# Weight halves at a step of 132 words, and matmuls that stream and write their columns from the last to the first

## The reference, cut to what matters

```python
# first block, per layer (DEPTH = 2)
proj = jnp.einsum('btd,de->bte', h, w_in[l])
c_out = ... jnp.einsum('btc,cd->btd', y, w_pw)
x = x + jnp.einsum('btd,de->bte', merged, w_out[l])
gu = jnp.einsum('btd,df->btf', h2, w_gate_up[l])
x = x + jnp.einsum('btf,fd->btd', jax.nn.silu(g) * up, w_down[l])
# second block
proj = h @ w_in
... (o * jax.nn.silu(g)) @ w_ret_o ; y @ w_sgu_o ; merged @ w_out
... h @ w_up ; conv ; (jax.nn.gelu(a) * b) @ w_down
```

## Time and profile before

| | |
|---|---|
| runs | 2197.36 and 2197.77 us, median 2197.57 |
| profiled execution | span 2195.6 us from the first to the last instruction; some 2.0 us of the runs' time lie around it |
| PE | 2182.7 us busy (99%), 10528 matmuls |
| PEld | 1813.8 us (83%) |
| DVE | 1378.5 us (63%) |
| ACT | 965.5 us (44%) |
| DMA | 27% of the 16 engines, 95 GB/s |
| granted TensorE clock | 0.999 of full speed |

### The profile page before, as it was taken

The page is one execution under the profiler, slowest core; times in us unless marked ns, Lnnn a source line. Parts: engine busy times, 40 slices in busy tenths (PEclk is TensorE's granted clock), DMA queues, the critical chain, the costliest instruction groups (busy, mean ns, idle before and its releaser), DMA issues.

```text
span 2195.6 us, 28930 instructions
## 1 busy us (share of the span) xinstructions
PE 2182.7 (99%) x10528; PEld 1813.8 (83%) x10528; DVE 1378.5 (63%) x1978; ACT 965.5 (44%) x1392; POOL 74.7 (3%) x103
## 2 busy tenths in 40 slices
PE   9999999999999999999999999999999999999998
PEld 6878888888888878888888888888888899888887
DVE  7999954444345999954444334654776568888723
ACT  5678544443223588544443223331554344333412
POOL 0000020000010000020000010000000000000000
PEclk9999999999999999999999999999999999999999
DMA  5221222222223211222222224223222231222222
GB/s 182 75 78 65 96 96 96 96 96 84 93 93 123 90 62 64 94 96 100 99 99 92 80 92 156 97 77 131 84 91 87 96 135 39 100 101 97 94 96 77
DMA packets 35397, 208.39 MB, mean 95 GB/s; under 512 B 4512, under 2 KB 5024, under 8 KB 14816
## 3 DMA queue, kind: packets, MB, share of 16 engines
q1 hardware_dynamic: 35296, 207.07, 27.0%
HBM read 201.15 MB, written 2.10 MB: 93 GB/s over the span
## 4 chain that ended last, share of the span: by engine, by line
PE 94%; ACT 3%; DVE 2%; issue 1%; DMA 0%; SPq 0%; DVEq 0%
PE mm L1794 25%; PE mm L1796 25%; PE mm L1795 25%; PE sp L1794 4%; PE sp L1795 4%; PE sp L1796 4%; PE sp L1896 1%; PE ob L1924 1%; DVE conv_y L1171 1%; ACT probs L584 1%; DVE probs L1201 1%; ACT probs L592 1%; PE sp L1911 0%; DMA x<-in_x_dram 0%; PE ob L1796 0%
## 5 line engine op out<-in xcount | busy, mean ns | idle before, releaser
L1794 PE MATMUL mm<-in_hi,w_hi 128*128 128x512 f32 (+1 forms) x1696 | 663.8, 391 | 3.8 <-DVE in_lo L1104 2.1
L1796 PE MATMUL mm<-in_hi,w_lo 128*128 128x512 f32 (+1 forms) x1696 | 657.0, 387 | 0.0
L1795 PE MATMUL mm<-in_lo,w_hi 128*128 128x512 f32 (+1 forms) x1696 | 657.0, 387 | 0.0
L525 ACT ACTIVATE w_hi<-w_raw 128x2048 fp32r<-128x2048 f32 (+3 forms) x193 | 346.2, 1794 | 674.8 <-PE mm L1796 557.9
L1070 DVE TENSOR_TENSOR w_lo<-w_raw,w_hi 128x2048 fp32r<-128x2048 f32 (+3 forms) x193 | 422.3, 2189 | 239.5 <-ACT w_hi L525 239.0
L1794 PEld LDWEIGHTS mm<-in_hi,w_hi 128*128 128x128 f32 x1696 | 318.5, 188 | 75.1 <-DVE in_lo L1104 6.0
L1796 PEld LDWEIGHTS mm<-in_hi,w_lo 128*128 128x128 f32 x1696 | 318.4, 188 | 65.8
L1795 PEld LDWEIGHTS mm<-in_lo,w_hi 128*128 128x128 f32 x1696 | 318.6, 188 | 64.1 <-issue 1.0
L1171 DVE SCALAR_TENSOR_TENSOR conv_y<-conv_in,parl,conv_y 128x512 f32<-128x512 f32 x240 | 170.0, 747 | 1.7
L1081 DVE TENSOR_TENSOR tB<-mm,rstd 128x512 f32<-128x512 f32 x54 | 37.3, 691 | 172.8 <-PE mm L1796 172.8
L1794 PE MATMUL mm<-act_hi,w_hi 128*128 128x512 f32 x352 | 136.9, 389 | 0.0
(11 more groups left out here) (429 smaller groups left out, 3257.0 us busy)
## 6 DMA issues: line engine op xcount, KB each, us to landing
w_raw<-in_w_dram SPq DMA_DIRECT2D x160, 1024.0 KB, 4.8
w_raw<-in_w_dram SPq DMA_DIRECT2D x32, 704.0 KB, 3.9
w_raw<-in_w_dram SPq DMA_DIRECT2D x5, 512.0 KB, 4.7
out_dram<-z_rows SPq DMA_DIRECT2D x8, 256.0 KB, 2.1
rope<-in_rope_dram SPq DMA_DIRECT2D x3, 512.0 KB, 3.6
x<-in_x_dram SPq DMA_DIRECT2D x4, 256.0 KB, 4.9
x<-in_x_dram SPq DMA_DIRECT2D x2, 512.0 KB, 7.9
sq<-ssum SPq DMA_DIRECT2D x32, 32.0 KB, 1.8
```

The source lines that it names most:

```text
L525: e.activation(whi[:, slot, 0:cols], raw[:, slot, 0:cols], ACT.Copy).then_inc(s_whi, whi_out.up())
L1794: MM(out, ah, bh, start=first, stop=False, **kw)
L1795: MM(out, ah, bl, start=False, stop=False, **kw)
L1796: return MM(out, al, bh, start=False, stop=last, **kw)
```

## The change

The high halves get a new layout: a weight tile is still 128 words, but one starts every 132 words (528 bytes). The low halves stay at 128 words per tile; they only get a dimension more in their shape. `w_hi` is thereby 512 bytes longer in each partition. The filler `to_512_bytes` (368 bytes) is gone. Together this moves `w_lo` by 512 bytes, and `in_hi`, `in_lo`, `act_hi`, `w_out` and all behind them from 128 to 256 bytes past a multiple of 512; `w_lo` stays at 128 past one, and the tiles of `w_hi` start at 128, 144, 160 and so on.

In `mm3` the moving operand and the output are both read with a step of -1: the last column streams first and is written to its own place. The result is in the same place as before. Matmuls outside `mm3` are unchanged. Every engine issues the same instructions in the same order (5130 rows of program on PE, 1461 on DVE, 702 on ACT, 163 on SP, in both); only their operands' address patterns differ. ACT and DVE read or write `w_hi` as runs of 128 words at a step of 132. Where the weights are the moving operand, `w_hi` is read in two or four such runs, backwards.

```diff
+WSTEP = P + 4
...
-        whi = sb("w_hi", [P, 2, CH], F32R)
-        wlo = sb("w_lo", [P, 2, CH], F32R)
+        whi = sb("w_hi", [P, 2, CH // P, WSTEP], F32R)
+        wlo = sb("w_lo", [P, 2, CH // P, P], F32R)
...
-        sb("to_512_bytes", [P, 92])
...
+        def w_cols(t, slot, a, b):
+            return t[:, slot, a // P:b // P, 0:P]
+        def w_tile(t, slot, k):
+            return t[:, slot, k, 0:P]
+        def raw_cols(slot, a, b):
+            return raw[:, slot, a:b].rearrange("p (k c) -> p k c", c=P)
...
-                e.activation(whi[:, slot, 0:cols], raw[:, slot, 0:cols], ACT.Copy).then_inc(s_whi, whi_out.up())
+                e.activation(w_cols(whi, slot, 0, cols), raw_cols(slot, 0, cols), ACT.Copy).then_inc(s_whi, whi_out.up())
...
-                TT(wlo[:, slot, first:cols], raw[:, slot, first:cols], r32(whi[:, slot, first:cols]),
+                TT(w_cols(wlo, slot, first, cols), raw_cols(slot, first, cols), r32(w_cols(whi, slot, first, cols)),
...
-                MM(out, ah, bh, start=first, stop=False, **kw)
-                MM(out, ah, bl, start=False, stop=False, **kw)
-                return MM(out, al, bh, start=False, stop=last, **kw)
+                back, bh, bl = (t[:, ::-1] if len(t.shape) == 2 else t[:, ::-1, ::-1] for t in (out, bh, bl))
+                MM(back, ah, bh, start=first, stop=False, **kw)
+                MM(back, ah, bl, start=False, stop=False, **kw)
+                return MM(back, al, bh, start=False, stop=last, **kw)
...
-                    a = slice((at + j) * P, (at + j + 1) * P)
-                    ins = mm3(four[bank], whi[:, slot, a], wlo[:, slot, a], hi_[:, k, :], lo_[:, k, :],
+                    ins = mm3(four[bank], w_tile(whi, slot, at + j), w_tile(wlo, slot, at + j), hi_[:, k, :], lo_[:, k, :],
...
-                    ws = slice(T * j, T * j + T)
-                    ins = mm3(four[wide_banks[b]], xh[:, k, ts], xl[:, k, ts], whi[:, slot, ws], wlo[:, slot, ws],
+                    ws = (slot, T * j, T * j + T)
+                    ins = mm3(four[wide_banks[b]], xh[:, k, ts], xl[:, k, ts], w_cols(whi, *ws), w_cols(wlo, *ws),
```

More of the change, by code:

```diff
@@ L533, in prep_part @@
             def prep_part(cs):
-                e.activation(whi[:, 0, cs], raw[:, 0, cs], ACT.Copy).then_inc(s_whi, whi_out.up())
+                e.activation(w_cols(whi, 0, cs.start, cs.stop), raw_cols(0, cs.start, cs.stop), ACT.Copy).then_inc(s_whi, whi_out.up())
             def prep_rest():
@@ L1115, in prep_and_sum @@
                 for cs in (slice(0, CH // 2), slice(CH // 2, CH)):
-                    TT(wlo[:, 1, cs], raw[:, 1, cs], r32(whi[:, 1, cs]), ALU.subtract).then_inc(s_w, w_out.up())
+                    TT(w_cols(wlo, 1, cs.start, cs.stop), raw_cols(1, cs.start, cs.stop),
+                       r32(w_cols(whi, 1, cs.start, cs.stop)), ALU.subtract).then_inc(s_w, w_out.up())
                     if cs.start == 0:
@@ L1136, in _ @@
             first_lo((2,))
-            more = slice(CH // 4, CH // 2)
             e.wait_ge(s_whi, whi_in.next())
-            TT(wlo[:, 0, more], raw[:, 0, more], r32(whi[:, 0, more]), ALU.subtract).then_inc(s_do, own.up())
+            TT(w_cols(wlo, 0, CH // 4, CH // 2), raw_cols(0, CH // 4, CH // 2), r32(w_cols(whi, 0, CH // 4, CH // 2)),
+               ALU.subtract).then_inc(s_do, own.up())
             first_lo((3,))
@@ L2011, in token_major @@
                         e.wait_ge(ready.sem, ready.next())
-                    ws = slice(256 * k, 256 * k + 256)
-                    ins = mm3(mm[bank][:, 0:256], xh[:, k, ts], xl[:, k, ts], whi[:, slot, ws], wlo[:, slot, ws],
+                    ws = (slot, 256 * k, 256 * k + 256)
+                    ins = mm3(mm[bank][:, 0:256], xh[:, k, ts], xl[:, k, ts], w_cols(whi, *ws), w_cols(wlo, *ws),
                               k == 0, k == KT - 1)
@@ L2122, in half_product @@
                         e.wait_ge(ready.sem, ready.next())
-                    a = slice(at + k * P, at + (k + 1) * P)
-                    ins = mm3(out, wh[:, a], wl[:, a], xh[:, k, hs], xl[:, k, hs], k == 0, k == KT - 1)
+                    ins = mm3(out, wh[:, at + k, 0:P], wl[:, at + k, 0:P], xh[:, k, hs], xl[:, k, hs], k == 0, k == KT - 1)
                 return ins
@@ L2136, in out_half @@
             def out_half(m, hs, ks=range(KT), ready=None):
-                return half_product(four[m % 4][:, 0:TH], wo[:, m // 2, 0, :], wo[:, m // 2, 1, :],
-                                    CH // 2 * (m % 2), hs, ready, ks)
+                wh, wl = (wo[:, m // 2, i, :].rearrange("p (k c) -> p k c", c=P) for i in range(2))
+                return half_product(four[m % 4][:, 0:TH], wh, wl, KT * (m % 2), hs, ready, ks)
             def up_half(j, hs, ks=range(KT), ready=None):
-                return half_product(four[j][:, hs], whi[:, j // 2, :], wlo[:, j // 2, :],
-                                    CH // 2 * (j % 2), hs, ready, ks)
+                return half_product(four[j][:, hs], whi[:, j // 2, :, :], wlo[:, j // 2, :, :],
+                                    KT * (j % 2), hs, ready, ks)
             e.wait_ge(s_w, w_in.next())
@@ L2192, in _ @@
                         e.wait_ge(s_mmf, taken.next())
-                        half_product(bank, whi[:, c, :], wlo[:, c, :], CH // 2 * d,
+                        half_product(bank, whi[:, c, :, :], wlo[:, c, :, :], KT * d,
                                      slice(0, T)).then_inc(s_mm, tiles.up())
@@ L2210, in rows_product @@
                     k = 2 * c + j
-                    ws = slice(j * D + d * T, j * D + d * T + T)
+                    ws = (c % 2, j * D + d * T, j * D + d * T + T)
                     ts = slice(b * P, (b + 1) * P)
@@ L2216, in rows_product @@
                         e.wait_ge(s_xe, 2 * b + d + 1)
-                    ins = mm3(rows[b][d], acth[:, k, ts], actl[:, k, ts], whi[:, c % 2, ws], wlo[:, c % 2, ws],
+                    ins = mm3(rows[b][d], acth[:, k, ts], actl[:, k, ts], w_cols(whi, *ws), w_cols(wlo, *ws),
                               k == 0, k == FT - 1)
```

## The result

| | before | changed |
|---|---|---|
| time (median) | 2197.57 us | 2256.78 us (2256.65 and 2256.91) |
| ratio | | 1.027, 95% interval 1.024 to 1.030 |
| profiled execution's span | 2195.6 us | 2254.9 us |

What follows compares the result with a forecast made beforehand. It took PE, busy 99% of the span, as the bound. From a 2195.6 us span, -63 for the reversed stream and +5 given back in the heads made 2137.6; with 2.0 around it, 2140 us, range 2100 to 2265.

Steps and rivals of the forecast that it cites:

- What bounds the kernel: Whole kernel: PE is busy 99% of the span, so only the time between matmul starts can move the time much.
- fixed extra for each matmul: In `mm3`: 13.3 ns beyond the columns' share at 512 and 256 columns alike, 127 us over 9504 matmuls, 5.8%.
- the reversed stream: In `mm3`, 9504 matmuls: pace falls from 226.67 to 220 ns, -63 us; bounds -127 us and, at 232 ns, +51 us.
- Giving the layout no term of its own: 132-word step and missing filler, same 9504 matmuls: part of the reversal's term, between the same ends; no term added.
- Rival C: In `mm3`: high weights at 528-byte steps never meet the stream alike; pace 232 ns, +51 us, 2248 us; chance 0.29.
- the forecast's own 2100 to 2190: Rival A, in `mm3`: gain by a better phase, up to four fifths of the extra, 2100 to 2190 us; chance 0.48.
- Rival B: In `mm3`: the 13.3 ns are the exchange of weights, the change doesn't reach them; 2197 us; chance 0.15.
- Rival D: In `mm3`: backward streams or writes run below one column per cycle; some 1900 us more, 4100 in all; chance 0.08.
- ACT and DVE at nothing: Writing and reading `w_hi` in runs of 128 words: 0 us for both, durations staying 1.92 and 2.29 us.
- Given back in the heads: In the heads a faster PE meets a nearly full DVE: 2.5 us lost in each of two stretches, +5 us.
- 256 columns: Sign in `mm3`: 256-column matmuls at about 113 ns, extra equal to 512's; 512 losing twice as much would mean rival D.
- The three lines of a triple: Sign in `mm3`: if high weights matter, the three matmul lines of a triple have different paces.

Runs made afterwards that it cites:

- single-tile groups: A program of its own, not the kernel: groups of 40 matmuls of one float32r tile, the stream's start moved by 16 bytes between groups; 226.7 ns at start 0 forward.
- the small program: A program of its own, not the kernel: groups of 60 matmuls of one tile, every fourth 16-byte line first, at all sixteen starts; 220.0 ns at start 4.

## Why the prediction was wrong, point by point

- **What bounds the kernel** was right: PE's pace alone moved the time. The 127 us that the pace's extra makes up were the right quantity to watch. The 213.33 and 106.7 ns that they leave to the columns are an estimate, though: 106.7 is the difference of the two paces at 512 and 256 columns, 226.67 - 120, and 213.33 twice that. No run shows 512 columns at 213.3 ns; the lowest settled pace measured is 220.0.
- **"The pace depends on how the weight load's reads meet the stream's reads"** was right, and the single-tile groups show it: 226.7 to 234.7 ns by the start alone, also when only the weight tile moves. That it is a "fixed extra for each matmul" was not: of the starts measured at both widths, start 0 alone has 13.3 ns in both. At start 12 the extra is 20 ns for 512 columns (233.4) and 6.8 for 256 (113.5), so the argument that an equal extra must come from the load's 128 columns was chance.
- **The step that failed is the sum's first term, the reversed stream, -63 us.** I took the middle of the good side on a guess, that a stream running beside the load keeps off it. Measured: backward at the unchanged start costs +6.67 ns, 50 us. A backward stream has the same extra of 20 ns (233.3) at fourteen of sixteen starts. My upper bound of 232 ns was too low as well; it came from a stretch on its way back to the settled pace, and 234.5 was measured. The guess on geometry had no row behind it; the runs don't show in which order the array takes its weights.
- **Giving the layout no term of its own** was the second failure. Alone it costs 38 us. Rival C came near in its number (2248 us against 2256.8), and that is largely luck: its mechanism, high weights at 132-word steps that never meet the stream alike, was measured with a forward stream at 2235, and there the missing filler alone costs 46 us and the step gives 8 back. The rest of the loss is the reversal's own, which C did not see. Its row was still the best witness on record: after one shift by 2 lines the next ten starts came at 232 ns each. I weighed that less than the wish that some other state might be better.
- **The range** of 2100 to 2265 us took in the 2256.8 only through C; the forecast's own 2100 to 2190 did not.
- **Rival B** is out: the extra does move with addresses (2243 us, 2% more, by a filler of 128 bytes alone), and with the order of the stream (2248 us).
- **Rival D** fell. A step of -1 is free inside lines (226.7 settled at start 0), and the write may go backward (226.7 too). Streams read and written in pieces of 4 words at every fourth line had 220.0 to 231 ns by their start, where the straight order has 226.7 to 234.7; only pieces of 2 words, which the change doesn't have, came to 431. No run shows a column per cycle, as its name has it; measured are 0.417 ns a column between 256 and 512.
- **ACT and DVE at nothing** was right: 1.92 and 2.29 us as before.
- **Given back in the heads**: the sign turned with the term. All else on PE took 2.9 us less, 2.4 of it where PE had waited for ACT.
- **256 columns**: I expected the extra to be equal in 256 and 512 columns. It is 11.6 against 21.1 ns: those of 512 lost 7.8 ns, those of 256 gained 1.7. A larger loss in the wide ones was to be the sign of D, and it was not D, so the test was badly chosen.
- **The three lines of a triple** were to have different paces if the high weights matter. They have 234.3, 234.8 and 234.4 ns where the weights are stationary, although the layout costs 38 us alone: this sign could not tell either.

## What to carry to other kernels

When PE is busy all the time, divide a long stretch by its matmuls: what stands above the columns' own share (0.417 ns each here, by the difference of 512 and 256 columns) is worth a search of its own. Its size depended here on where the moving operand starts with respect to the weights, modulo 256 bytes (226.7 to 234.7 ns), and on the order of the stream's 16-byte lines (220.0 to 278 ns). A filler in front of an operand is a change of 2% here (2243 against 2197 us). Measure start and order in a small program first, read the real addresses of the operands in the kernel, and trust only its own trace, since it can settle at another pace than the small program did (223.3 in one stretch where the small program had 220.0).

## What the runs showed of the hardware that I had not expected

- The pace is a state, not a number: the same matmuls settle at 220.0 in one stretch and 223.3 in another of the same execution, and go through ten others (224 to 236 ns) after a disturbance before they settle. A settled pace is a sequence of times between starts that repeats: 227, 227, 226; or 225, 222; or 234, 229, 220, 224, 227.
- Pieces of 2 words at every fourth line cost 431 to 438 ns a matmul, about twice the usual 226.7: with pieces of 4 words (one line) it is 220 to 231.
- Four sweeps of every fourth line can be below the straight order (220.0 at the best starts against 226.67, but 230 to 231 at starts 5 and 6), sixteen are far above (277 to 278). Which property of the memory makes 4 good was not tried.
- The best settled pace seen, 220.0 ns, is still 6.7 ns above 512 columns at 0.417 ns each, an estimate from the earlier trace rows. Whether that rest can be moved stays open.
